# One index column per slot: when GpSimd copies its indices and issues its gathers

## The chip, the cores and the metric

The kernel runs on one core of one Trainium2 chip. The metric is the device time of one execution, in microseconds. Three runs of the kernel before gave a median of 1371.26 us, from 1369.24 to 1378.64. TensorE is called PE below, VectorE DVE, ScalarE ACT, GpSimd POOL and SyncE SP.

## The reference, cut to what matters

The program is one inference step of an encoder layer on 384 tokens (256 of a prompt, 8 streams of 16): a norm, a projection, an mLSTM group beside a sparse attention group, an output projection, and then an expert retrieval, in which the change lies:

```
qp = (x @ w_pq).reshape(T, PEER_HEADS, 2, D_PKEY // 2)
s = jnp.einsum('thcd,hcnd->thcn', qp, subkeys).astype(f32)
s1, i1 = lax.top_k(s[:, :, 0], PEER_TOPK)
s2, i2 = lax.top_k(s[:, :, 1], PEER_TOPK)
...
top_s, sel = lax.top_k(cand, PEER_TOPK)
eidx = jnp.take_along_axis(cidx, sel, axis=-1)
g = jax.nn.softmax(top_s, axis=-1)
u = pu[eidx]
vv = pv[eidx]
a = jax.nn.gelu(jnp.einsum('thkd,td->thk', u, x).astype(f32))
return jnp.einsum('thk,thkd->td', (g * a).astype(vv.dtype), vv)
```

There are 8 heads with 16 experts each, so 128 experts a token, of 16384. A token needs 128 rows of u and 128 rows of v, 1024 floats each.

## The kernel before, in words

The tokens stand in three tiles of 128, one token per partition, taken in the order 2, 0, 1. Everything up to the first routing takes the first 360 us. Then each tile goes through 16 rounds of 8 slots. A slot (`slots[s]`, 128 partitions by 2048 floats) takes, by one indirect DMA, one expert row for each of the 128 tokens, u beside v, 8 KB each, from `peer_uv` in HBM. There are 8 slots, and one gather fills each slot in each round: 3 x 16 x 8 = 384 gathers.

What happens to a slot, by engine:

- POOL copies the indices from `eidx` into a small tile, and issues the gather (`gather`, lines 555 to 577). Its descriptors are made by POOL's software.
- DVE waits for the landing and makes the dot of u with the token, line 1499, `experts`. Between the rounds of the first tile and at the start of the second, DVE also does the routing of later heads and tiles (`routing_steps`: searches on lines 1432 to 1442, pairs, expert indices on lines 1471 to 1492). A step stands behind a round's eight dots, in program order.
- ACT makes the gelu (L731), multiplies by the gate (L733) and writes a diagonal matrix of the weights (L736), and counts `diag_ok`.
- PE waits for the diagonal and multiplies it with the v half, 4 matmuls per slot in float32 as the profile counts them (L1068), accumulating in two banks; it counts `used`. In the first tile's rounds PE also makes the queries of the other two tiles (L1060) and their scores (L1042, L1051).

After a tile's 16 rounds, DVE adds the sum to the residual, norms it (L1505 to L1512), and SP writes it out.

The order of POOL's work is that of its program: `gather` is called for the very first round with `first=True`, unrolled, and then in a loop over rounds. In it stand two groups of four slots (HALF = 4). A group begins with a wait for `diag_ok`, the fourth diagonal of the same group one round ago; by then the issue of the four old gathers, which read the same index tile, is long past. Then one copy of four columns into `isl[g]` follows, and a wait for that copy. Then for each slot come a wait for `used` (the slot's matmuls of the round before), a product of one column by zeros into `pad`, and the issue. In the first round the waits are for the banks' last uses of the memory in which the slots lie (`slot_after`).

Of the kernel before, what the change touches and what calls it, by code (L numbers as in the profile page):

```python
# [12 lines left out]
U32 = mybir.dt.uint32  # L13
ALU = mybir.AluOpType
# [29 lines left out]
SLOTS = 8  # L44
HALF = SLOTS // 2
ROUNDS = HK // SLOTS
# [98 lines left out]
def encoder_kernel(nc, d):  # L145

    plan = psum_plan()
    index = {n: i for i, (n, _) in enumerate(plan)}
    assert len(index) == len(plan)
    CC, NCONST = const_columns()  # L150

    with ExitStack() as ctx:
# [3 lines left out]
        def sem(name):  # L156
            return ctx.enter_context(nc.semaphore(name))

        def at(lo, *shape, parts=P, p0=0):
            n = 1  # L160
            for s in shape:
                n *= s
            assert lo + n <= 52992
            v = arena[p0:p0 + parts, lo:lo + n]
            names = "abcd"[:len(shape)]
            if len(shape) > 1:
                v = v.rearrange(f"p ({' '.join(names)}) -> p {' '.join(names)}",
                                **{c: s for c, s in zip(names[1:], shape[1:])})
            return v

        def over(ap, dim, n):

            v = ap.unsqueeze(dim)
            shape = list(v.shape)
            shape[dim] = n
            return v.broadcast_to(shape)
# [37 lines left out]
        o = CONST + NCONST  # L214
# [81 lines left out]
        o = SM  # L296
# [12 lines left out]
        eidx = at(o + 2176, NT, HK).bitcast(U32)  # L309
        aslot = at(o + 2560, SLOTS)  # L310
        gslot = at(o + 2568, SLOTS)
        wslot_e = at(o + 2576, SLOTS)
        isl = [at(o + 2584 + HALF * g, HALF).bitcast(U32) for g in range(2)]
        pad = at(o + 2592, 1 + SLOTS)
        diag = at(o + 2608, SLOTS, P)
        o += 2608 + SLOTS * P
        assert o <= wslot_at[3]
# [3 lines left out]
        slot_after = ["y11"] * 4 + ["qq3"] * 2 + ["qq7"] * 2  # L321
        slots = [at(a, 2 * DM) for a in slot_at]
# [59 lines left out]
        hn_ok = sem("hn_ready")  # L382
        idx_ok = sem("experts_ready")
        isl_ok = sem("index_slots_ready")
        landed = [sem(f"row_landed_{s}") for s in range(SLOTS)]
        used = sem("rows_used")
        a_ok = sem("dots_ready")
# [2 lines left out]
        diag_ok = sem("diagonals_ready")  # L390
# [4 lines left out]
        def n_read(name, eng):  # L395
            return sum(e == eng for _, e in plan[:index[name] + 1])

        def filled(eng, name):

            eng.wait_ge(filled_s, index[name] + 1)  # L400

        def was_read(eng, name):

            e = plan[index[name]][1]
            eng.wait_ge(read_v if e == "V" else read_a, n_read(name, e))
# [96 lines left out]
        @block.gpsimd  # L502
        def _(pool):
            chain = [0]

            def link(ins):
                chain[0] += 1
                ins.then_inc(p_chain, 1)
                pool.wait_ge(p_chain, chain[0])

            nc.gpsimd.memset(qbd, 0.0)
            nc.gpsimd.memset(qibd, 0.0).then_inc(zeros_p, 1)
            nc.gpsimd.memset(mv1[:, :, :, DH:DX], 1.0).then_inc(mv_ones, 1)
            was_read(pool, "xT21")
            filled(pool, "xT21")
            nc.gpsimd.memset(qdf, 0.0).then_inc(zeros_p, 1)

            pool.wait_ge(mv_ones, 1)
            was_read(pool, "mv2")
            pool.wait_ge(wkm_ok, 1)  # L520
            pool.wait_ge(state_in, 16)
            for h in range(HM):
                if h:
                    filled(pool, f"CN{h - 1}2")
                for t in range(2):
                    nc.gpsimd.tensor_tensor(vw[:, NB + t, :], mv1[:, t, h, :],  # L526
                                            cols[:, 2, t, h:h + 1].broadcast_to([P, DX]), ALU.mult)
                nc.gpsimd.tensor_tensor(vw[:, 0:NB, :], over(mv1[:, 2, h, :], 1, NB),
                                        over(wkm[:, h, :], 2, DX), ALU.mult).then_inc(vw_ok, 1)
                filled(pool, f"NUM{h}")  # L530
                was_read(pool, "decay")
                nc.gpsimd.tensor_tensor(CT[:, h], CT[:, h], over(decb[:, h, :], 2, DX), ALU.mult).then_inc(ct_ok, 1)  # L532

            pool.wait_ge(ml_done, 1)
            nc.gpsimd.memset(kbd, 0.0)
            nc.gpsimd.memset(pnf, 0.0).then_inc(pn0_ok, 1)
            link(nc.gpsimd.memset(ikbd, 0.0))
            was_read(pool, "small")
            was_read(pool, "ak3")

            pool.wait_ge(kidx_in, 16)
            nc.gpsimd.tensor_copy(kiT2[:, :, PAST:LK],
                                  ikT2[:, PROMPT:T].rearrange("p (b t) -> p b t", b=NB)).then_inc(kt_ok, 1)
            pool.wait_ge(cache_in, 16 * JP)
            nc.gpsimd.tensor_copy(KT[:, :, :, PAST:LK],
                                  akT[:, :, PROMPT:T].rearrange("p j (b t) -> p j b t", b=NB)).then_inc(kt_ok, 1)
            pool.wait_ge(kt_ok, 2)

            for e in range(2):
                r = slice(64 * e, 64 * e + 64)  # L550
                link(nc.gpsimd.tensor_copy(ikbd[r, e, :], ikT2[r, 0:PROMPT]))
                nc.gpsimd.tensor_copy(kbd[r, :, e, :], akT[r, :, 0:PROMPT]).then_inc(kbd_ok, 1)
                pool.wait_ge(kbd_ok, e + 1)


            def gather(n, t, i, first):

                done = n * ROUNDS + i
                for g in range(2):
                    if not first:  # L560

                        pool.wait_ge(diag_ok, done * SLOTS - SLOTS + HALF * g + HALF)
                    nc.gpsimd.tensor_copy(isl[g], eidx[:, t, bass.ds(i * SLOTS + HALF * g, HALF)]).then_inc(isl_ok, 1)  # L563
                    pool.wait_ge(isl_ok, done * 2 + g + 1)
                    for s in range(HALF):
                        if first:
                            if slot_after[HALF * g + s]:
                                filled(pool, slot_after[HALF * g + s])
                        else:

                            pool.wait_ge(used, done * SLOTS - SLOTS + HALF * g + s + 1)

                        k = 1 + HALF * g + s
                        nc.gpsimd.tensor_tensor(pad[:, k:k + 1], pad[:, 0:1], pad[:, 0:1], ALU.mult)  # L574
                        nc.gpsimd.indirect_dma_start(  # L575
                            slots[HALF * g + s], None, d["peer_uv"],
                            bass.IndirectOffsetOnAxis(ap=isl[g][:, s:s + 1], axis=0)).then_inc(landed[HALF * g + s], 16)

            for n, t in enumerate(ORDER):
                for part, (u, head, heads) in enumerate(PARTS):  # L580
                    if u != t:
                        continue
                    pool.wait_ge(idx_ok, part + 1)
                    if part == 0:
                        link(nc.gpsimd.memset(pad[:, 0:1], 0.0))  # L585
                        gather(n, t, 0, True)
                    per_head = PK // SLOTS
                    with pool.Fori(max(head * per_head, int(part == 0)), (head + heads) * per_head) as i:
                        gather(n, t, i, False)
# [1074 lines left out]
```

## Time and profile before

| | |
|---|---|
| median of three runs | 1371.26 us (1369.24 to 1378.64) |
| profiled execution | 1376.4 us, of which the span of instructions is 1374.6 us |
| PE busy | 1155.5 us, 84% |
| DVE busy | 799.4 us, 58% |
| ACT busy | 463.8 us, 34% |
| POOL busy | 678.0 us, 49%, 898 instructions |
| gathers (queue of software DMAs) | 402.68 MB of 454.86 MB |

Busy time is time in which an instruction of the engine runs; waits, semaphore and register instructions are not in it. Shares are of the whole span and average over stages that differ. "Idle before" is idle time of the engine just ahead of an instruction, with the one whose end seems to have released it. PEclk is the clock that was granted to PE, 1.00 for its high level of 2.4 GHz, 0.50 for the low one of 1.2 GHz. The DMA share is the mean over the core's 16 DMA engines; it can come out slightly above 1.

### The profile page before, as it was taken

How to read it: one execution, taken by the hardware profiler on the slowest of the kernel's cores; microseconds unless marked ns; L12 is line 12 of the kernel's file. 1: busy time of each engine (PE TensorE's matmuls, PEld its weight loads, DVE VectorE, ACT ScalarE, POOL GpSimd, SP SyncE). 2: the span in 40 equal slices, each digit the busy share in tenths (PEclk: the TensorE clock that was granted, in tenths of full speed). 3: DMA queues.
4: the chain of work that ended last, by engine and by line, in shares of the span. 5: the costliest groups of instructions: out<-in, count | busy, mean ns of one | idle time of the engine just before them, and what ended most of it. 6: DMA issues, size and time to landing. Idle time of an engine off the chain costs nothing.

```text
span 1374.6 us, 12457 instructions
## 1 busy us (share of the span) xinstructions
PE 1155.5 (84%) x3320; PEld 557.0 (41%) x3320; DVE 799.4 (58%) x1837; ACT 463.8 (34%) x1355; POOL 678.0 (49%) x898
## 2 busy tenths in 40 slices
PE   6999899999999997778767778788777877777776
PEld 4546555577855553333323333222222322222222
DVE  4005534866656777878778786455555544455444
ACT  2101200320242433433324343443444444444443
POOL 0002112000255556566655666767776777767772
PEclk9999999989999999798997889999998999999999
DMA  8321528432489999999998999999999999999996
GB/s 316 120 80 62 105 52 295 190 130 116 172 341 384 373 378 422 374 421 386 403 421 338 421 374 407 417 417 422 422 422 422 423 422 422 422 413 422 422 421 268
DMA packets 68825, 454.86 MB, mean 331 GB/s; under 512 B 7241, under 2 KB 14765, under 8 KB 17329
## 3 DMA queue, kind: packets, MB, share of 16 engines
q0 software_dynamic: 55296, 402.68, 71.2%
q1 hardware_dynamic: 12656, 48.60, 10.3%
q10 hardware_dynamic: 832, 3.08, 0.7%
q8 instruction: 20, 0.33, 0.1%
q14 instruction: 21, 0.16, 0.0%
HBM read 446.62 MB, written 7.71 MB: 331 GB/s over the span
## 4 chain that ended last, share of the span: by engine, by line
PE 36%; DMA 30%; POOL 12%; issue 9%; DVE 8%; ACT 4%; POOLq 1%; DVEq 0%; ACTq 0%; SPq 0%
DMA arena<-in_peer_uv,arena 29%; PE ps L1068 10%; PE ps L802 7%; POOL arena L575 7%; PE ps L808 4%; PE ps L1060 4%; POOL arena L574 3%; PE ps L922 3%; POOL arena L563 2%; PE ps L1042 2%; DVE arena L1499 2%; ACT arena L736 1%; ACT arena L733 1%; PE ps L1015 1%; DVE arena L1261 1%
## 5 line engine op out<-in xcount | busy, mean ns | idle before, releaser
L1068 PE MATMUL ps<-arena 128*128 128x512 f32 x1536 | 755.9, 633 | 190.6 <-ACT arena L736 190.4
L1499 DVE CUSTOM_DVE_ANT_0 arena<-arena 128x1024 f32<-128x1024 f32 x384 | 468.1, 1231 | 374.3 <-DMA arena<-in_peer_uv,arena 373.4
L1068 PEld LDWEIGHTS ps<-arena 128*128 128x128 f32 x1536 | 285.7, 198 | 655.6 <-ACT arena L736 369.0
L575 POOL DMA_INDIRECT arena<-in_peer_uv,arena x384 | 445.5, 1160 | 85.9 <-issue 76.9
L731 ACT ACTIVATE arena<-arena 128x1 f32<-128x1 f32 x384 | 77.3, 201 | 469.4 <-DVE arena L1499 466.1
L563 POOL COPY arena<-arena 128x4 uint32 (+1 forms) x96 | 71.9, 749 | 223.6 <-ACT arena L736 223.2
L736 ACT ACTIVATE arena<-arena 128x128 f32<-128x128 f32 x384 | 154.2, 402 | 12.5
L574 POOL TENSOR_TENSOR arena<-arena 128x1 f32<-128x1 f32 x384 | 132.3, 344 | 34.2 <-POOL arena L563 14.5
L733 ACT ACTIVATE arena<-arena 128x1 f32 (+1 forms) x384 | 113.0, 294 | 32.5
L802 PE MATMUL ps<-arena 128*128 128x384 f32 (+1 forms) x336 | 112.2, 492 | 0.0
L616 ACT ACTIVATE arena<-ps 128x512 f32<-128x512 f32 (+2 forms) x63 | 30.6, 511 | 239.5 <-PE ps L1060 70.7
L802 PEld LDWEIGHTS ps<-arena 128*128 128x128 f32 (+1 forms) x336 | 63.5, 192 | 44.0 <-issue 2.2
L585 POOL MEMSET arena<- 128x1 f32 x1 | 0.1, 98 | 140.9 <-DVE arena L1488 140.9
L808 PE MATMUL ps<-arena 128*128 128x512 f32 x144 | 62.5, 592 | 0.0
L1060 PE MATMUL ps<-arena 128*128 128x256 f32 x256 | 56.2, 379 | 0.9 <-ACT arena L616 0.9
L526 POOL TENSOR_TENSOR arena<-arena 128x129 f32<-128x129 f32 x8 | 3.0, 401 | 106.8 <-DVE arena L1189 88.7
L1060 PEld LDWEIGHTS ps<-arena 128*128 128x128 f32 x256 | 48.6, 190 | 9.4 <-issue 1.9
L922 PE MATMUL ps<-arena 128*128 128x512 f32 x96 | 43.3, 603 | 1.6 <-ACT arena L616 1.6
L731 ACT ACT_TABLE_LOAD x33 | 42.3, 1283 | 0.6
L808 PEld LDWEIGHTS ps<-arena 128*128 128x128 f32 x144 | 27.1, 190 | 32.8 <-issue 32.5
L532 POOL TENSOR_TENSOR arena<-arena 128x1032 f32<-128x1032 f32 x4 | 7.6, 1909 | 62.9 <-PE ps L886 62.9
L1499 DVE DVE_READ_ACCUMULATOR2_ANT arena<- 128x1 f32 x384 | 30.5, 80 | 0.0
(230 smaller groups left out, 710.1 us busy)
## 6 DMA issues: line engine op xcount, KB each, us to landing
arena<-in_w_in SPq DMA_DIRECT2D x8, 2048.0 KB, 7.6
arena<-in_w_pq SPq DMA_DIRECT2D x4, 2048.0 KB, 9.9
arena<-in_peer_uv,arena POOLq DMA_INDIRECT x384, 9.6
arena<-in_w_out SPq DMA_DIRECT2D x3, 1024.0 KB, 7.0
arena<-in_state_C ACTq DMA_DIRECT2D x1, 2064.0 KB, 10.3
out_new_C_s<-arena SPq DMA_DIRECT2D x1, 2064.0 KB, 6.6
arena<-in_cache_k SPq DMA_DIRECT2D x4, 512.0 KB, 7.0
arena<-in_cache_v SPq DMA_DIRECT2D x1, 2048.0 KB, 16.5
```

What stands on the lines that cost most here:

```text
L563: nc.gpsimd.tensor_copy(isl[g], eidx[:, t, bass.ds(i * SLOTS + HALF * g, HALF)]).then_inc(isl_ok, 1)
L574: nc.gpsimd.tensor_tensor(pad[:, k:k + 1], pad[:, 0:1], pad[:, 0:1], ALU.mult)
L575: nc.gpsimd.indirect_dma_start(slots[HALF * g + s], None, d["peer_uv"], bass.IndirectOffsetOnAxis(ap=isl[g][:, s:s + 1], axis=0)).then_inc ...
L731: act.activation(gslot[:, s:s + 1], aslot[:, s:s + 1], ACT.Gelu_apprx_tanh).then_inc(ge_ok, 1)
L733: act.activation(wslot_e[:, s:s + 1], gflat[:, t, bass.ds(i * SLOTS + s, 1)], ACT.Copy, scale=gslot[:, s:s + 1]).then_inc(w_ok, 1)
L736: act.activation(diag[:, s, :], ident, ACT.Copy, scale=wslot_e[:, s:s + 1]).then_inc(diag_ok, 1)
L802: last = mm(b[0:m, 0:T], w[:, k, lo:lo + m], xnT[:, k, :], start=k == 0, stop=k == KC - 1)
L808: last = mm(b, xnT[:, k, P * t:P * t + P], w[:, k, :], start=k == 0, stop=k == KC - 1)
L922: last = mm(b, mixT[:, k, P * t:P * t + P], wout[i][k], start=k == ks[0], stop=k == ks[-1])
L1060: last = mm(b[:, 0:PROMPT], w[:, k, P * g:P * g + P], xnT[:, k, 0:PROMPT], start=k == 0, stop=k == KC - 1)
L1068: last = mm(ps[:, BANKS + half, :], diag[:, s, :], slots[s][:, DM + 512 * half:DM + 512 * half + 512], start=first and s == 0, stop=final ...
L1499: v.tensor_tensor_reduce(slots[s][:, 0:DM], slots[s][:, 0:DM], hn[:, t, :], 1.0, 0.0, ALU.mult, ALU.add, aslot[:, s:s + 1]).then_inc(a_ok, 1)
```

## The change

The two index tiles of four columns become eight of one column, one for each slot. The zero column `pad` and its products are gone, with the memset that fills it. In `gather` the group level disappears: each slot waits for its own `used` count, then copies its one column, waits for that copy, increments a new semaphore that nobody waits for, and issues its gather. The wait for `diag_ok` is gone from POOL. In the first round the order is the same, behind `slot_after`.

```diff
-        isl = [at(o + 2584 + HALF * g, HALF).bitcast(U32) for g in range(2)]
-        pad = at(o + 2592, 1 + SLOTS)
+        isl = [at(o + 2584 + s, 1).bitcast(U32) for s in range(SLOTS)]
...
+        issued = sem("gathers_begun")
...
-                done = n * ROUNDS + i
-                for g in range(2):
-                    if not first:
-
-                        pool.wait_ge(diag_ok, done * SLOTS - SLOTS + HALF * g + HALF)
-                    nc.gpsimd.tensor_copy(isl[g], eidx[:, t, bass.ds(i * SLOTS + HALF * g, HALF)]).then_inc(isl_ok, 1)
-                    pool.wait_ge(isl_ok, done * 2 + g + 1)
-                    for s in range(HALF):
-                        if first:
-                            if slot_after[HALF * g + s]:
-                                filled(pool, slot_after[HALF * g + s])
-                        else:
-
-                            pool.wait_ge(used, done * SLOTS - SLOTS + HALF * g + s + 1)
-
-                        k = 1 + HALF * g + s
-                        nc.gpsimd.tensor_tensor(pad[:, k:k + 1], pad[:, 0:1], pad[:, 0:1], ALU.mult)
-                        nc.gpsimd.indirect_dma_start(
-                            slots[HALF * g + s], None, d["peer_uv"],
-                            bass.IndirectOffsetOnAxis(ap=isl[g][:, s:s + 1], axis=0)).then_inc(landed[HALF * g + s], 16)
+
+                done = (n * ROUNDS + i) * SLOTS
+                for s in range(SLOTS):
+                    if first:
+                        filled(pool, slot_after[s])
+                    else:
+                        pool.wait_ge(used, done - SLOTS + s + 1)
+                    nc.gpsimd.tensor_copy(isl[s], eidx[:, t, bass.ds(i * SLOTS + s, 1)]).then_inc(isl_ok, 1)
+                    pool.wait_ge(isl_ok, done + s + 1)
+                    pool.sem_inc(issued, 1)
+                    nc.gpsimd.indirect_dma_start(
+                        slots[s], None, d["peer_uv"],
+                        bass.IndirectOffsetOnAxis(ap=isl[s], axis=0)).then_inc(landed[s], 16)
...
-                        link(nc.gpsimd.memset(pad[:, 0:1], 0.0))
```

## Rows read from the trace of the kernel before

**Rows 1.** Stretches: bounds, length, busy us per engine, PEclk, DMA share, GB/s.

```profile
500.00:860.00 360.00, 281.12 (x600) 118.98 (x598) 279.46 (x769) 136.58 (x421) 220.97 (x308) 0.88 0.97 397
860.00:1340.00 480.00, 381.22 (x769) 132.12 (x770) 242.58 (x392) 204.94 (x603) 345.19 (x434) 0.99 1.01 421
```

**Rows 2.** Timeline around 1200 us, DVE and PE: start, duration, what, idle before.

```profile
1200.21 1.23 DVE L1499 CUSTOM_DVE_ANT_0 arena<-arena 128x1024 f32<-128x1024 f32 x1 [1.24 <-DMA arena<-in_peer_uv,arena]
...
1202.59 1.98 PE L1068 MATMUL ps<-arena 128*128 128x512 f32 x4 [0.50 <-ACT arena L736]
...
1205.17 1.23 DVE L1499 CUSTOM_DVE_ANT_0 arena<-arena 128x1024 f32<-128x1024 f32 x1 [1.24 <-DMA arena<-in_peer_uv,arena]
```

**Rows 3.** Chain of waits in order of time, 448 to 485 us: start, us, what.

```profile
448.48 14.00 PE ps L1068 x32
462.48 6.92 PE ps L1060 x32
470.72 14.00 PE ps L1068 x32
```

**Rows 4.** Stretches of 10 us with low DMA share, columns as in rows 1.

```profile
490.00:500.00 10.00, 8.14 (x29) 4.72 (x28) 7.75 (x13) 7.30 (x23) 2.30 (x4) 1.00 0.77 321
560.00:570.00 10.00, 10.00 (x23) 4.46 (x22) 8.60 (x19) 5.60 (x13) 8.53 (x12) 0.94 0.73 269
730.00:740.00 10.00, 10.00 (x23) 4.38 (x22) 9.82 (x21) 6.81 (x16) 8.59 (x10) 0.91 0.44 164
```

**Rows 5.** Timeline at 366 us and around 1200 us, POOL.

```profile
366.13 0.19 POOL L563 COPY arena<-arena 128x4 uint32<-128x4 uint32 x1
...
1200.51 1.78 POOL L575 DMA_INDIRECT arena<-in_peer_uv,arena  x1 [0.15 <-issue]
...
1205.19 1.25 POOL L563 COPY arena<-arena 128x4 uint32 x1 [1.55 <-ACT arena L736]
1206.61 0.20 POOL L574 TENSOR_TENSOR arena<-arena 128x1 f32<-128x1 f32 x1 [0.16 <-POOL arena L563]
1207.27 0.98 POOL L575 DMA_INDIRECT arena<-in_peer_uv,arena  x1 [0.47 <-issue]
```

**Rows 6.** Page, costliest groups, POOL's: count, busy us, mean ns, idle before.

```profile
L575 POOL DMA_INDIRECT arena<-in_peer_uv,arena x384 | 445.5, 1160 | 85.9 <-issue 76.9
...
L563 POOL COPY arena<-arena 128x4 uint32 (+1 forms) x96 | 71.9, 749 | 223.6 <-ACT arena L736 223.2
...
L574 POOL TENSOR_TENSOR arena<-arena 128x1 f32<-128x1 f32 x384 | 132.3, 344 | 34.2 <-POOL arena L563 14.5
```

**Rows 7.** One tile's instructions: the gathers from 900 to 1300 us.

```profile
DMA to landing us min/median/max: 7.1/8.5/11.9
```

**Rows 8.** Stretch of 1 us at 558 us, columns as in rows 1.

```profile
558.00:559.00 1.00, 1.00 (x2) 0.34 (x1) 1.00 (x1) 0.87 (x3) 0.00 (x0) 0.50 1.04 434
```

**Rows 9.** Timeline around the low slice at 560 us.

```profile
555.56 16.80 PE L1068 MATMUL ps<-arena 128*128 128x512 f32 x32 [8.50 <-ACT arena L736]
559.13 13.22 PE L1068 MATMUL ps<-arena 128*128 128x512 f32 x28
...
559.11 1.16 POOL L563 COPY arena<-arena 128x4 uint32 x1 [7.85 <-ACT arena L736]
560.17 1.23 DVE L1499 CUSTOM_DVE_ANT_0 arena<-arena 128x1024 f32<-128x1024 f32 x1
560.43 1.02 POOL L574 TENSOR_TENSOR arena<-arena 128x1 f32<-128x1 f32 x1 [0.16 <-POOL arena L563]
561.60 0.98 POOL L575 DMA_INDIRECT arena<-in_peer_uv,arena  x1
```

**Rows 10.** Timeline around 732 us, POOL.

```profile
733.03 1.80 POOL L575 DMA_INDIRECT arena<-in_peer_uv,arena  x1
```

**Rows 11.** Timeline around 667 us, POOL.

```profile
667.05 1.49 POOL L575 DMA_INDIRECT arena<-in_peer_uv,arena  x1 [1.79 <-issue]
```

**Rows 12.** Stretch of 10 us at 660 us, columns as in rows 1.

```profile
660.00:670.00 10.00, 10.00 (x21) 4.24 (x20) 6.39 (x11) 4.90 (x16) 4.51 (x8) 0.83 0.96 388
```

## The prediction

> **What bounds the kernel now.** I read the time by stretches first. From 860 to 1340 us the DMA engines are busy at 1.01 and move 421 GB/s, while PE, DVE and POOL have idle time; from 500 to 860 us it is 0.97 and 397 GB/s [rows 1]. A gather moves 128 rows of 8 KB, 1.049 MB; at 421 GB/s that is 2.49 us. The starts of DVE's dots confirm it: two dots later is 4.96 us, 2.48 us each [rows 2]. So the last third is bound by the transfers. In the chain of waits the rounds from about 380 to 492 us are PE's instead: 14.0 us of expert matmuls, 6.92 us of prompt queries, and round again after 22.2 us, where eight gathers need 19.9 us [rows 3]. Between 490 and 860 us both are interrupted by routing work on DVE: there the reader should see five slices of 10 us in which the DMA share is only 0.44 to 0.79 (three of them are shown) [rows 4]. The missing rate is (421 - 397) / 421 x 360 us = 20.5 us from 500 to 860 us, and (421 - 321) / 421 x 10 = 2.4 us in the slice from 490: 23 us is all that better feeding of the transfers can give.
>
> **What POOL does.** In the bound stage a gather takes 1.79 us of POOL's 2.49 (345.19 us of 480 [rows 1], over 193 gathers). The group's copy starts when ACT's fourth diagonal is there; the product and the issue follow [rows 5]. The issue takes 0.97 us, or 1.78 us when it begins inside a DVE dot: the issue that began at 1200.51 ended 0.85 us after the dot that ended at 1201.44. The copy that began at 1205.19 ended at 1206.44, with the dot of 1205.17 to 1206.40 [rows 2, 5]. So each POOL instruction that meets a dot waits for its end. The Trainium skill (SBUF — State Buffer, two separate sides) says the same more strongly: VectorE with two SBUF inputs and a GpSimd operation that reads SBUF take one port pair as an exclusive lock. By that rule alone all products, copies and issues would wait whenever DVE is busy; here issues beside DVE's searches still take 0.97 us, so the dots are what counts.
>
> **The change, part by part.** The sum is against the profiled execution (1376.4 us, span 1374.6), which lies 5 us above the median of the runs, 1371.3; I take the difference from the median.
>
> (1) Removed: 384 products, mean 344 ns, 132 us of POOL [rows 6]. Added: 288 more copies (384 instead of 96). No copy of one column is in the trace. The nearest row is the product of one column, 0.20 us free of a dot [rows 5]; the copy of four columns takes 0.19 us free and 1.25 us in a dot [rows 5], mean 749 ns [rows 6]. I take 0.20 free and the rest of the dot where it meets one, since it has the same shape as the product. One copy then replaces one product and the old copies drop out: POOL's work falls slightly. In the bound stage this is worth nothing, POOL not being the limit; the transfers cover it. Bounds: 0 to the price of rival A.
>
> (2) Each copy is now awaited before its issue: 0.17 us from copy to product and 0.46 us from product to issue at the group's head [rows 5]. I put both on every gather: 0.20 + 0.63 + 0.98 = 1.81 us of POOL, plus at most the rest of one dot. The increment of the new semaphore has no row; between 0 and the 0.46 us gap, taken inside that gap. Does POOL keep up? A dot takes 1.23 us of the 2.48; the freed slot comes 4.36 us after its dot's start (dot from 1200.21, matmuls from 1202.59 to 1204.57 [rows 2]), which is 1.88 us into the next dots' period. The copy ends at 2.2, the issue begins at 2.5 to 2.9, waits for the dot to 3.7 (1.23 of the next period), and ends at 4.6, 0.85 later. That is 2.1 into the next period: the next slot's copy starts there, and the same repeats. POOL locks to the period and does not stretch it. The slot is out of the queue for 4.4 + 2.7 = 7.1 us of 19.9, so about five gathers stay queued. Time from issue to landing, 8.5 us now [rows 7], should rise to about 12. The stage gains and loses 0 us.
>
> (3) The new copy waits for its own slot's matmuls instead of the fourth diagonal. Queued behind that wait are only the later slots' copies and gathers, which become free in the same order. Nobody but the gathers waits for POOL here. In the PE stage the transfers have slack already: 0, unless PE's cover goes, and it is 2.3 us a round (22.2 - 19.9). The part that can pay is the holes. A hole begins when all eight slots have landed and DVE is still in a routing step; no slot is free, so earlier issuing can't move its start. Its end can move. In the hole at 560 us the PE clock is granted at 0.50 [rows 8], its low level of 1.2 GHz, after PE had been idle for 8.5 us, so slot 0's four matmuls, begun at 555.56, end only about when the fifth begins, at 559.13. The old copy, released by the fourth diagonal, starts at 559.11 [rows 9]. The old wait thus costs nothing; what goes is the product of 1.02 us. New: copy until 560.25, issue begun at 560.45 to 560.75 inside the dot of 560.17 to 561.40, ended 0.85 later at 562.25, against 561.60 + 0.98 = 562.58 [rows 9]: 0.35 us. The holes of 644 and 816 us have the same pattern, that of 498 (PE warm) gives about 0.5. In the long one at 730 us copy and product each met a dot, and the issue of 733.03 met a third and took 1.80, to 734.83 [rows 10]; without the product the issue meets the dot before and ends at about 733.7: 1.1 us. Slots 1 to 7 follow at PE's 1.7 us, faster than 2.48, so they change nothing. Sum 3 x 0.35 + 0.5 + 1.1 = 2.7 us. Bounds for these: 0, and all 23 us.
>
> (4) At 667 us a thin stretch: slot 1's issue begins 1.79 us late by the row, share 0.96 in that slice [rows 11, 12]. With that row's gap gone, 1.3 us (388 of 421 GB/s for two such slices gives 1.6 at most). First gather of all: product and memset gone, 0.3 us earlier at 360 us, under PE's rounds, 0.
>
> Sum: -2.7 - 1.3 = **-4.0 us**, so 1367 us (profiled execution 1372). What a measurement can tell from no change is about 1%, 13.7 us; this is below it.
>
> **The rivals.** A: **POOL becomes the limit**, slower. Place: every gather after 500 us. With the means of today, copy 0.749, waits 0.17 + 0.46, issue 1.160 [rows 5, 6], a gather takes 2.54 us of POOL, 0.055 above the transfers' 2.48; over about 330 gathers +18 us, 1390 us. If copy and issue each met a whole dot it would be 1.25 + 0.63 + 1.78 = 3.66 us, but a longer period has more free time, so that can't hold. The point from which it decides is 2.48 us of POOL per gather. Against it: the phases of part 2, where only one of the two meets a dot. For it: an unseen cost of waits on the sequencer. The Trainium skill (GPSIMD Engine Reference, Performance pitfalls for Q7 kernels) speaks against the change: many small reads, one per gather index, should be batched, since each pays about 102 cycles; its estimate is 288 x 85 ns = 24 us of POOL. The trace agrees in kind: a product of one column takes as long as a copy of four, 0.20 and 0.19 us [rows 5]; but POOL has the time. Chance of A 0.12.
>
> B: **the deeper queue fills the holes**, faster. If the holes came from slots that sat free behind the group's fourth diagonal (up to 3 x 2.48 = 7.4 us), most of the 23 us would return: 1348 with all, 1356 with two thirds. For it: POOL's idle time before the copies is charged to ACT's diagonals, 223 us [rows 6]. Against: in the holes all eight slots are landed, and the low clock delays the first free one. Chance 0.13.
>
> C: **nothing changes**, 1371, the wait for the slot having always been the later one where it counts; it lies in the forecast's band. Forecast with C: 0.75.
>
> **How the numbers follow.** Forecast and C spread over 1362 to 1376, with the runs' own spread (1369 to 1379) to 1380. The range reaches to B's 1356 and to part of A: 1356 to 1384. Faster by over 1% (below 1357.5) 0.12, slower by over 1% (above 1385) 0.11, within 1% 0.77.
>
> **What would show it.** 384 copies of about 0.2 or up to 1.2 us and no product; POOL waiting for PE's matmuls, not for diagonals; issue to landing near 12 us; DMA share still 1.01 from 900 us on, dots 2.48 us apart; the five holes at their old places and hardly shorter. I am wrong if dots in the last stage are further apart than 2.5 us (A), if POOL has no idle time there, or if the slices of 0.44 and 0.73 fill up (B).

## The result, and the profile after

The changed kernel is slightly slower. 17 runs of it have a median of 1384.06 us (1376.51 to 1391.11); 17 of the kernel before, in the same jobs, 1375.59 us (1369.24 to 1379.74). The ratio is 1.0065, 95% interval [1.0043, 1.0087]: +0.65%, about 9 us. The forecast was -4 us, within 1% of no change. It was right that the change is small; the sign was wrong, and the median lies just above the upper end of the range, 1384. Part of the distance to the forecast of 1367 us is the starting point: it was taken from three runs with a median of 1371.3, and the 17 runs lie in two clusters, eight from 1369.2 to 1371.7 and eight from 1377.6 to 1379.7, with one between them that happens to be the median.

The profiled execution of the changed kernel took 1378.85 us, span 1377.0, close to the one of before. The two spans compare badly, because the work ahead of the gathers, which nobody changed, was faster in it. The reader should measure from the first gather's issue to DVE's addition at the end of each tile. In the changed kernel (start, duration, what):

```profile
353.61 1.14 POOL L568 DMA_INDIRECT arena<-in_peer_uv,arena  x1 [0.96 <-POOL arena L565]
...
717.95 0.69 DVE L1497 TENSOR_TENSOR arena<-arena,ps 128x512 f32<-128x512 f32 x1
...
1044.69 0.69 DVE L1497 TENSOR_TENSOR arena<-arena,ps 128x512 f32<-128x512 f32 x1 [3.16 <-PE ps L1060]
...
1369.50 0.69 DVE L1497 TENSOR_TENSOR arena<-arena,ps 128x512 f32<-128x512 f32 x1 [3.16 <-PE ps L1060]
```

And in the kernel before:

```profile
360.89 1.16 POOL L575 DMA_INDIRECT arena<-in_peer_uv,arena  x1 [0.43 <-issue]
...
720.32 0.69 DVE L1505 TENSOR_TENSOR arena<-arena,ps 128x512 f32<-128x512 f32 x1
...
1046.83 0.69 DVE L1505 TENSOR_TENSOR arena<-arena,ps 128x512 f32<-128x512 f32 x1 [3.16 <-PE ps L1068]
...
1367.00 0.69 DVE L1505 TENSOR_TENSOR arena<-arena,ps 128x512 f32<-128x512 f32 x1 [3.16 <-PE ps L1068]
```

Before, the three tiles take 359.4, 326.5 and 320.2 us, 1006.1 in all. After, they take 364.3, 326.7 and 324.8 us, 1015.9 in all. The gather phase is 9.8 us longer, the size of the difference of the medians; it is lost in the first and the last tile.

The stretches that answer to [rows 1] show less moved in both:

```profile
500.00:860.00 360.00, 274.23 (x590) 115.09 (x588) 275.13 (x738) 136.52 (x421) 210.24 (x270) 0.90 0.97 393
860.00:1340.00 480.00, 378.30 (x763) 131.03 (x764) 239.21 (x388) 203.18 (x597) 317.76 (x381) 0.99 1.01 417
```

393 in place of 397 GB/s, and 417 in place of 421 in a stage that the transfers should bound. The page's groups of POOL answer to [rows 6]:

```profile
L568 POOL DMA_INDIRECT arena<-in_peer_uv,arena x384 | 432.6, 1127 | 318.6 <-POOL arena L565 162.8
...
L565 POOL COPY arena<-arena 128x1 uint32 (+1 forms) x384 | 186.0, 484 | 203.1 <-DVE arena L1480 135.7
```

POOL is less busy than before (646.9 us for 678.0), yet idle time of 318.6 us has appeared in front of the issues, where it was 85.9. It is 0.83 us a gather. It is time between the end of the copy and the start of the issue, and it is no spare time: POOL cannot use it. The steady state around 1201 us, which answers to [rows 2] and [rows 5]:

```profile
1201.08 0.96 POOL L568 DMA_INDIRECT arena<-in_peer_uv,arena  x1 [0.81 <-PE ps L1060]
1201.38 1.98 PE L1060 MATMUL ps<-arena 128*128 128x512 f32 x4 [0.49 <-ACT arena L728]
1201.50 1.23 DVE L1491 CUSTOM_DVE_ANT_0 arena<-arena 128x1024 f32<-128x1024 f32 x1 [1.26 <-DMA arena<-in_peer_uv,arena]
1202.04 0.72 POOL L565 COPY arena<-arena 128x1 uint32 x1
...
1203.57 0.95 POOL L568 DMA_INDIRECT arena<-in_peer_uv,arena  x1 [0.81 <-PE ps L1060]
```

The copy starts the moment the last issue ends (1201.08 + 0.96 = 1202.04), so its slot had been free already. The copy meets the dot and ends with it (1202.76 against 1202.73). Then 0.81 us pass, then the issue. 0.72 + 0.81 + 0.96 = 2.49 us: POOL has no slack at all, though its least time is 0.19 + 0.81 + 0.96 = 1.96 us. As forecast it has locked to the dots' period. What the forecast missed is what this means: a POOL that makes exactly one issue per dot never makes up for a delay by itself.

The delays can be seen in the time from issue to landing, which the text takes as the depth of the queue (min, median, max of the gathers between 900 and 1300 us, then between 900 and 920, 940 and 960, 1210 and 1230):

```profile
DMA to landing us min/median/max: 5.5/7.8/9.9
...
DMA to landing us min/median/max: 9.3/9.3/9.4
...
DMA to landing us min/median/max: 6.8/6.8/6.8
...
DMA to landing us min/median/max: 5.5/5.8/5.9
```

It was forecast to rise from 8.5 to 12 us; it fell to 7.8. It mostly stays at one level for tens of us and drops at single places, from 9.3 to 6.8 us at 943 and from 7.8 to 5.8 at 1211. Between them it came back to 7.8: by 980 us, behind a slice of 10 us at 388 GB/s, and again by 1260, behind the slices at 393 and 380 shown below. So the depth does come back, but while it does the transfers lose time. The two drops come from a pause in front of an issue:

```profile
1207.02 0.71 POOL L565 COPY arena<-arena 128x1 uint32 x1
1211.12 0.96 POOL L568 DMA_INDIRECT arena<-in_peer_uv,arena  x1 [3.39 <-PE ps L1060]
1212.08 0.68 POOL L565 COPY arena<-arena 128x1 uint32 x1
1213.59 0.96 POOL L568 DMA_INDIRECT arena<-in_peer_uv,arena  x1 [0.82 <-PE ps L1060]
```

3.39 us in place of 0.81. It stands before gathers number 114, 220 and 326 of 384. The kernel before has a shorter pause before numbers 114 and 326 too ([rows 11] is the first; the second is 1.48 us). There POOL had slack: the slice from 1210 us fell to 388 GB/s, and the next four are at 421 to 426. Here the queue is down to 5.8 us afterwards, and the transfers run thin:

```profile
1230.00:1240.00 10.00, 7.54 (x16) 2.41 (x14) 4.78 (x8) 3.57 (x12) 6.74 (x9) 1.00 1.01 408
1240.00:1250.00 10.00, 7.93 (x16) 2.71 (x16) 4.97 (x8) 4.04 (x12) 6.74 (x9) 1.00 1.00 393
1250.00:1260.00 10.00, 6.57 (x14) 2.41 (x15) 4.27 (x7) 3.55 (x12) 6.74 (x9) 1.00 1.00 380
```

With the two slices before them (370 and 402 GB/s) that is (52 + 20 + 14 + 29 + 42) / 422 x 10 = 3.7 us. The kernel before loses 0.7 us in the same five slices, so this stretch explains about 3 us of the last tile's 4.6. The share of each tile differs from one execution to the next: in the trace of e6 below, the changed kernel with its loop written out, the three tiles take 363.4, 327.9 and 322.1 us.

In the first tile the refill after a hole is a part of it. The one that answers to [rows 9]:

```profile
550.00 16.92 PE L1060 MATMUL ps<-arena 128*128 128x512 f32 x32 [8.50 <-ACT arena L728]
...
553.95 0.76 POOL L565 COPY arena<-arena 128x1 uint32 x1 [6.79 <-PE ps L1060]
...
555.52 1.15 POOL L568 DMA_INDIRECT arena<-in_peer_uv,arena  x1 [0.81 <-POOL arena L565]
...
557.78 1.35 POOL L568 DMA_INDIRECT arena<-in_peer_uv,arena  x1 [0.81 <-POOL arena L565]
...
570.31 1.13 POOL L568 DMA_INDIRECT arena<-in_peer_uv,arena  x1 [0.81 <-POOL arena L565]
```

The first issue stands 5.52 us after PE's start, where it was 6.04 (555.56 to 561.60): 0.5 us gained, as forecast (0.35). But the seventh issue is at 570.31, six spacings of 2.47 us; before, all eight were out from 561.60 to 574.09, seven spacings of 1.78. The queue is refilled no faster than the transfers drain it. The slices from 550 to 590 us are at 298, 382, 398 and 380 GB/s, 5.5 us short of 422; before, the two slices at 269 and 409 from 560 us were 3.9 us short.

### The profile page after: what moved, and what is told of

Same layout as the page of the kernel before. It is cut to its first block, busy times and chain, and to the rows that moved or that the text cites. A ratio compares the mean times of both kernels' runs of the same rounds, so it can differ in the third digit from the quotient of the medians.

```text
span 1377.0 us, 13306 instructions
## 1 busy us (share of the span) xinstructions
PE 1147.1 (83%) x3320; PEld 549.6 (40%) x3320; DVE 796.3 (58%) x1837; ACT 463.7 (34%) x1355; POOL 646.9 (47%) x801
## 4 chain that ended last, share of the span: by engine, by line
PE 37%; DMA 20%; POOL 16%; DVE 11%; issue 11%; ACT 4%; POOLq 2%; SPq 0%; ACTq 0%; DVEq 0%
DMA arena<-in_peer_uv,arena 18%; PE ps L1060 12%; POOL arena L568 12%; PE ps L794 7%; PE ps L800 4%; POOL arena L565 4%; PE ps L1052 4%; DVE arena L1491 4%; PE ps L914 3%; PE ps L1034 2%; ACT arena L728 1%; DMA arena<-in_w_out 1%; ACT arena L725 1%; DVE arena L1253 1%; DVE arena L1475 1%
## 5 line engine op out<-in xcount | busy, mean ns | idle before, releaser
L568 POOL DMA_INDIRECT arena<-in_peer_uv,arena x384 | 432.6, 1127 | 318.6 <-POOL arena L565 162.8
L565 POOL COPY arena<-arena 128x1 uint32 (+1 forms) x384 | 186.0, 484 | 203.1 <-DVE arena L1480 135.7
L1034 PE MATMUL ps<-arena 128*128 128x128 f32 x256 | 29.3, 275 | 0.7 <-ACT arena L608 0.7
```

The costliest lines, as they stand in the source:

```text
L565: nc.gpsimd.tensor_copy(isl[s], eidx[:, t, bass.ds(i * SLOTS + s, 1)]).then_inc(isl_ok, 1)
L568: nc.gpsimd.indirect_dma_start(slots[s], None, d["peer_uv"], bass.IndirectOffsetOnAxis(ap=isl[s], axis=0)).then_inc(landed[s], 16)
L1034: last = mm(b[:, P * g:P * g + P], w[:, k, P * g:P * g + P], xnT[:, k, PROMPT:T], start=k == 0, stop=k == KC - 1)
```

## Experiments

Theory 1: an awaited small instruction directly ahead of each issue costs 0.81 us, so POOL needs 1.97 us a gather where it needed 1.35, and locked to DVE's dots it cannot refill the queue. Theory 2: the slot by slot order is what hurts. Theory 3: only the stages ahead differ. Each kernel was timed beside the kernel before, and ratios are to it.

The 1.35 us of theory 1 can be read in the kernel before, from one issue to the next inside a group (1199.16 to the issue of [rows 5] at 1200.51):

```profile
1199.16 0.97 POOL L575 DMA_INDIRECT arena<-in_peer_uv,arena  x1 [0.15 <-issue]
1200.15 0.21 POOL L574 TENSOR_TENSOR arena<-arena 128x1 f32<-128x1 f32 x1
```

**e2: the kernel before, with each product awaited.**

```diff
-                        nc.gpsimd.tensor_tensor(pad[:, k:k + 1], pad[:, 0:1], pad[:, 0:1], ALU.mult)
+                        nc.gpsimd.tensor_tensor(pad[:, k:k + 1], pad[:, 0:1], pad[:, 0:1], ALU.mult).then_inc(pad_ok, 1)
+                        pool.wait_ge(pad_ok, done * SLOTS + k)
+                        pool.sem_inc(issued, 1)
```

> The kernel before, with each product awaited (its own semaphore) before the issue behind it; the grouped wait for the diagonals and the grouped copies stay. Theory 1 (each gather's awaited small instruction puts 0.81 us between itself and the issue, so POOL needs at least 0.20 + 0.81 + 0.96 = 1.97 us a gather where it needed 1.35, and cannot catch up after a disturbance): slower than before by 5 to 12 us, about as the changed kernel or a little more, since the issues also begin late. Theory 2 (what costs is the earlier, slot by slot issue, through another phase against DVE's dots or a shallower queue): within 3 us of before. Theory 3 (the runs differ by the stages ahead of the gathers only): within 3 us.

1400.93 us, ratio 1.0184 [1.0131, 1.0237], +25 us. Nothing of the order was changed, and it is slower than the changed kernel. The sign is theory 1's, the size two to five times the 5 to 12 us that I wrote. A likely reason, not tested by itself: the copies of four stand beside the 384 awaited products here, and the issues of a group still begin late. POOL's rows show the same 0.81 us:

```profile
1101.38 0.97 POOL L579 DMA_INDIRECT arena<-in_peer_uv,arena  x1 [0.81 <-POOL arena L576]
1102.35 0.80 POOL L576 TENSOR_TENSOR arena<-arena 128x1 f32<-128x1 f32 x1
1103.96 0.97 POOL L579 DMA_INDIRECT arena<-in_peer_uv,arena  x1 [0.81 <-POOL arena L576]
```

**e3: the changed kernel, with the grouped wait put back.**

```diff
+                        if s % HALF == 0:
+                            pool.wait_ge(diag_ok, done - SLOTS + s + HALF)
                         pool.wait_ge(used, done - SLOTS + s + 1)
```

> The changed kernel, with the wait for the group's fourth diagonal put back ahead of the first and fifth slot of each round; one awaited copy per slot stays. Theory 1: as slow as the changed kernel or slower, +8 to +20 us over before, since late bursts are then issued at 1.97 us or more each. Theory 2: the grouping is what kept before fast, so this comes back to before, within 3 us. Theory 3: within 3 us.

1382.39 us, ratio 1.0062 [1.0029, 1.0095]: equal to the changed kernel. Theory 2 is out: the late order does not bring the time back. Theory 3 is out by this run, by e2 and by the length of the gather phase above. Nor does the early order give anything here that can be measured.

**e4: the kernel before without its product.**

```diff
-                        k = 1 + HALF * g + s
-                        nc.gpsimd.tensor_tensor(pad[:, k:k + 1], pad[:, 0:1], pad[:, 0:1], ALU.mult)
+                        pool.sem_inc(issued, 1)
```

> The kernel before without its 384 products and the zero column; a semaphore increment stands in their place, grouped copies and grouped waits stay. The issue has about 0.15 to 0.2 us less or one dot less before it. Theory 1: POOL needs about 1.1 us a gather, so equal to before or faster by up to 5 us. Theory 2: equal to before within 3 us. If the product itself were of use (it spaces the issues), slower by 5 us or more.

1372.59 us, ratio 0.9988 [0.9962, 1.0015]: no change. Taking the product out and putting the increment in comes to nothing that can be measured.

**e1: no copy at all.** POOL's loop is written out, and the gather reads its indices from the table.

```diff
-                    nc.gpsimd.tensor_copy(isl[s], eidx[:, t, bass.ds(i * SLOTS + s, 1)]).then_inc(isl_ok, 1)
-                    pool.wait_ge(isl_ok, done + s + 1)
                     pool.sem_inc(issued, 1)
...
-                        bass.IndirectOffsetOnAxis(ap=isl[s], axis=0)).then_inc(landed[s], 16)
+                        bass.IndirectOffsetOnAxis(ap=eidx[:, t, i * SLOTS + s:i * SLOTS + s + 1], axis=0)).then_inc(landed[s], 16)
...
-                    with pool.Fori(max(head * per_head, int(part == 0)), (head + heads) * per_head) as i:
+                    for i in range(max(head * per_head, int(part == 0)), (head + heads) * per_head):
```

> The changed kernel with POOL's loops over rounds written out, so that each gather reads its indices straight from the table of all indices: no copy, no wait for it; the issue waits only for its slot's matmuls. Theory 1: POOL needs about 1.0 to 1.2 us a gather, five gathers are queued, time from issue to landing rises to about 12 us, and the time falls below the kernel before by 3 to 8 us (about 1366). Theory 2 (early issue costs): +5 to +12 us over before, as the changed kernel. Theory 3: equal to before within 3 us.

1373.86 us, ratio 0.9994 [0.9966, 1.0022]. The awaited copy's cost is gone, with the slot by slot order kept, as theory 1 says. The further gain of 3 to 8 us did not come, although the queue filled up:

```profile
DMA to landing us min/median/max: 7.8/14.7/15.9
```

14.7 us of queue in place of 8.5 is worth nothing where 8.5 was already enough. This trace shows one thing more: its issues wait for PE, and they too start 0.8 us after what they wait for. PE's matmuls from 1142.25 end at 1144.23, the issue begins at 1145.05. So the 0.81 us is not special to a copy; but in the changed kernel it comes behind POOL's own work, on every gather.

**e5: each copy made one round ahead.** As many small copies as in the changed kernel (57 a half tile for 64), but the one an issue needs was made a round earlier.

```diff
-                    nc.gpsimd.tensor_copy(isl[s], eidx[:, t, bass.ds(i * SLOTS + s, 1)]).then_inc(isl_ok, 1)
-                    pool.wait_ge(isl_ok, done + s + 1)
+                    if (i + 1) % (4 * PK // SLOTS):
+                        copy_ahead(n, t, i + 1, s, 1)
+                    pool.wait_ge(isl_ok, ready[r, s])
                     pool.sem_inc(issued, 1)
```

> The changed kernel with POOL's rounds written out, two sets of eight index columns, and each copy made one round ahead of its gather (one copy of eight columns at the head of each half tile). As many small copies as in the changed kernel, each slot still issued as soon as it is free, but no issue stands behind a copy that has just been made. Theory 1 (the 0.81 us between an awaited small instruction and the issue): POOL needs about 0.20 + 0.15 + 0.96 = 1.3 us, issue to landing at 10 us or more, time equal to the kernel before within 3 us. Theory 2b (it is the number of small copies and their meetings with DVE's dots, not the awaiting): +5 to +10 us over before.

1373.67 us, ratio 1.0005 [0.9984, 1.0026], issue to landing 14.7 us. So it is the awaiting directly ahead of the issue, not the number of copies. Its timeline shows the same pause as above, and then what the changed kernel lacks:

```profile
1194.04 0.19 POOL L561 COPY arena<-arena 128x1 uint32<-128x1 uint32 x1
1197.25 1.76 POOL L580 DMA_INDIRECT arena<-in_peer_uv,arena  x1 [3.02 <-issue]
1199.02 0.19 POOL L561 COPY arena<-arena 128x1 uint32<-128x1 uint32 x1
1199.37 0.96 POOL L580 DMA_INDIRECT arena<-in_peer_uv,arena  x1 [0.15 <-issue]
1200.33 0.38 POOL L561 COPY arena<-arena 128x1 uint32<-128x1 uint32 x1
1200.87 0.96 POOL L580 DMA_INDIRECT arena<-in_peer_uv,arena  x1 [0.16 <-issue]
...
1202.18 1.80 POOL L580 DMA_INDIRECT arena<-in_peer_uv,arena  x1 [0.15 <-issue]
```

After the pause the next issues follow 2.12, 1.50 and 1.31 us apart, 0.15 us behind their neighbours' copies, and the delay is made up: issue to landing falls to 12.1 us and is back at 14.7 by 1210.

**e6: the changed kernel with POOL's loops written out**, the control for e1 and e5.

```diff
-                    nc.gpsimd.tensor_copy(isl[s], eidx[:, t, bass.ds(i * SLOTS + s, 1)]).then_inc(isl_ok, 1)
+                    nc.gpsimd.tensor_copy(isl[s], eidx[:, t, i * SLOTS + s:i * SLOTS + s + 1]).then_inc(isl_ok, 1)
...
-                    with pool.Fori(max(head * per_head, int(part == 0)), (head + heads) * per_head) as i:
+                    for i in range(max(head * per_head, int(part == 0)), (head + heads) * per_head):
```

> The changed kernel with POOL's loops written out and nothing else: the copies stay, each awaited before its issue. It is the control for the two kernels without loops. Theory 1: as the changed kernel, +6 to +11 us over before, issue to landing near 7.8 us, 0.8 us between copy and issue. If the loop (its branches and register waits) were what costs: equal to before within 3 us.

1383.11 us, ratio 1.0069 [1.0037, 1.0101]: the changed kernel's time. The loop is not the cause.

**e7: a second awaited instruction** between copy and issue.

```diff
                     pool.wait_ge(isl_ok, done + s + 1)
+                    nc.gpsimd.tensor_tensor(pad[:, 1 + s:2 + s], pad[:, 0:1], pad[:, 0:1], ALU.mult).then_inc(pad_ok, 1)
+                    pool.wait_ge(pad_ok, done + s + 1)
                     pool.sem_inc(issued, 1)
```

> The changed kernel with a second awaited small instruction (a product of one column) between copy and issue. POOL's least time a gather goes from 1.97 us to 0.20 + 0.16 + 0.20 + 0.81 + 0.96 = 2.33 us, or 2.98 us if the second wait costs 0.81 us as well. Theory 1: slower again, +20 to +40 us over before in the first case, and about 300 x (2.98 - 2.48) = +150 us in the second, since POOL then is the limit. Theory 2 (early issue or its phase is what costs): as the changed kernel, +6 to +11 us.

1434.27 us by the median, ratio 1.0486 [1.0423, 1.0549]: 60 us slower by medians, 67 by the ratio. The four runs spread widely, from 1410.39 to 1448.30 us, and the trace is that of the fastest. The rows show the first case (issue to issue 2.26 to 2.28 us at the least), since the first wait's successor is a product and starts after 0.08 us; only the issue stands 0.81 us behind:

```profile
1103.26 0.20 POOL L567 COPY arena<-arena 128x1 uint32 x1
1103.54 0.19 POOL L569 TENSOR_TENSOR arena<-arena 128x1 f32<-128x1 f32 x1
1104.55 1.19 POOL L572 DMA_INDIRECT arena<-in_peer_uv,arena  x1 [0.81 <-POOL arena L569]
```

The traced run is 37 us above the median of the kernel before, inside the expected 20 to 40; the three others are 60 to 74 us above, so the size was underestimated. POOL's least time of 2.28 us is still below the transfers' 2.48. The loss grows steeply as the distance between the two shrinks, as far as two points can say it: about 9 us at a least time of 1.97, 37 to 74 at 2.28. The least time alone does not set the loss, though: e2, whose issues inside a group stand 1.99 us apart at the least, lost 25 us. In its first stretch the rate is down to 368 GB/s:

```profile
500.00:860.00 360.00, 258.27 (x548) 107.37 (x547) 267.18 (x728) 127.78 (x395) 236.16 (x379) 0.87 0.96 368
```

**e8, e9 and their repeats: short dots.** In both kernels DVE's dot is cut to 256 columns (a part of the result is left out).

```diff
-                    v.tensor_tensor_reduce(slots[s][:, 0:DM], slots[s][:, 0:DM], hn[:, t, :], 1.0, 0.0,
+                    v.tensor_tensor_reduce(slots[s][:, 0:256], slots[s][:, 0:256], hn[:, t, 0:256], 1.0, 0.0,
```

> The changed kernel with DVE's dots cut to 256 of 1024 columns (the rest of each dot is left out), so a dot takes about 0.4 us in place of 1.23 and seldom holds POOL up. To be compared with the next run, the kernel before cut in the same way. Theory 1, with the dots holding POOL: POOL needs 1.97 us and has 0.5 us a gather to catch up, issue to landing rises to 12 us or more, and the difference between the two cut kernels shrinks from about 9 us to 0 to 4 us. If the awaited copy costs in some other way that has nothing to do with the dots: the difference stays at 7 us or more.

> The kernel before with DVE's dots cut to 256 of 1024 columns in the same way. All theories: a few us faster than the whole kernel before (the holes under DVE's routing are shorter by 0.8 us a slot), 1350 to 1368 us; the transfers bound both. Theory 1: the changed kernel cut in the same way lies 0 to 4 us above this one; otherwise 7 us or more.

> The changed kernel with dots cut to 256 of 1024 columns once more, on the same chip as the kernel before cut in the same way, so that the two are compared directly. Theory 1: 0 to 4 us above it. Otherwise 7 us or more above it.

The changed kernel cut: 1367.22 us, ratio 0.9954 [0.9927, 0.9980] (e8), and 1367.47, 0.9945 [0.9922, 0.9968] (e8b). The kernel before cut (e9): 1361.94, 0.9888 [0.9836, 0.9940], of four runs only. The medians of e8b and e9 are 5.5 us apart: between the two expectations. The traces say where. From 860 to 1340 us both move 422 GB/s, and both take 320.5 to 320.7 us for the last tile, where the whole kernels differ by 4.6. The changed kernel's queue, cut, is 15.1 us deep, that of the kernel before 10.8. In e8b:

```profile
1195.80 0.18 POOL L565 COPY arena<-arena 128x1 uint32 x1 [0.53 <-PE ps L1060]
...
1199.37 0.96 POOL L568 DMA_INDIRECT arena<-in_peer_uv,arena  x1 [3.39 <-issue]
...
1201.35 0.95 POOL L568 DMA_INDIRECT arena<-in_peer_uv,arena  x1 [0.82 <-PE ps L1060]
...
1203.31 0.96 POOL L568 DMA_INDIRECT arena<-in_peer_uv,arena  x1 [0.81 <-POOL arena L565]
```

With a dot of 0.43 us, the issues follow the pause 1.98 and 1.96 us apart: POOL's least time, below 2.48, so the delay is made up (issue to landing falls to 12.6 us and is back at 15.1 by 1210). The pair with more rounds:

> The kernel before with dots cut to 256 of 1024 columns, once more with more rounds, beside the changed kernel cut alike. So far the two lay 5.5 us apart by medians, of 4 and 10 runs; in their last tile both take 320.5 us, and both move 422 GB/s from 860 us on. Theory 1 as it stands (the dots' hold on POOL is what keeps the queue low in the last stage; the slow refill of 1.97 us a gather after each hole costs without them too): a difference of 2 to 6 us remains, all of it before the last tile. If all of the cost hung on the dots: 0 to 2 us.

> The changed kernel with dots cut to 256 of 1024 columns, in the same job. Theory 1 as it stands: 2 to 6 us above the run before this one, issue to landing near 15 us, last tile as long as there. If all of the cost hung on the dots: 0 to 2 us above.

1360.77 us, 0.9893 [0.9861, 0.9924] (e9b, before), and 1363.14 us, 0.9917 [0.9893, 0.9942] (e8c, changed): 2.4 us apart by medians, in the expected 2 to 6. So about 2 to 6 us are left with short dots, against about 9 with whole ones. How the 9 us divide is not settled, since the intervals of the two cut kernels overlap in both jobs. From the first gather's issue to the last addition, which leaves out the work ahead, the two traces of the kernel before, cut, have 997 us and the three of the changed kernel 998 to 1000: 1 to 3 us apart, against 9.8 for the whole kernels. Shown is that the last tile's part goes. That it goes because the dots no longer hold POOL is argued from the spacing of the issues: a short dot also frees its slot 0.8 us earlier, and no run separates the two.

No kernel here that computes the whole result beats the kernel before by more than the measurement can tell. e1, e4 and e5 are level with it.

## Why the prediction was wrong

**Step (1), right.** POOL is less busy with 384 copies than with products and old copies together: 646.9 for 678.0 us. e4 shows that taking the product out is worth nothing.

**Step (2) is the step that failed.** Its arithmetic was that POOL locks to the period, does not stretch it, and that therefore "about five gathers stay queued". The lock came, the queue did not, and the term "the stage gains and loses 0 us" measured +4.6 us in the last tile. I had computed one steady cycle as if each copy found its slot just freed. The real cycle has POOL behind: from 860 to 1340 us 188 of 190 copies start as soon as the issue before them ends, and the depth of the queue is what the last disturbance left, 9.3, 6.8 or 5.8 us, or the 7.8 to which it came back while the transfers lost time. A second fault made it worse: I took the gap to the issue as 0.17 + 0.46 = 0.63 us and left out the 0.20 of the product that ran inside it in [rows 5]. From the copy's end to the issue's start that row reads 0.83, and 0.81 is what every gather now pays. More important, [rows 5] and the rows of the kernel before under the experiments show that the gap is paid at the head of a group alone (0.47 us ahead of that issue, 0.15 ahead of one inside a group), so that the kernel before could issue every 1.35 us. This spare speed, 1.35 against 2.48, is what the change spent. e2 shows the loss with the awaiting alone, e1 and e5 show it gone without.

**Step (3), half right.** PE's idle time in the hole did not change (8.50 us in both), the first issue came 0.5 us earlier where 0.35 was forecast, and the first slot did come late with PE's clock granted at 0.50. "Slots 1 to 7 follow at PE's 1.7 us" was wrong: they follow at POOL's 2.47 us. This hole and its refill cost about 1.5 us more than before, and the first tile, where a gain of 2.7 us was forecast for the holes, took 4.9 us more.

**Step (4), wrong.** The 1.79 us pause of [rows 11] belongs to gather number 114, not to the grouping. It stayed, at 3.40 us, so the 1.3 us did not come.

**What holds POOL.** The prediction took the rule of the Trainium skill (SBUF — State Buffer, two separate sides) to mean that POOL waits whenever DVE is busy, and concluded that only the dots count. The rule names DVE instructions with two SBUF inputs (or in a two-port mode), and the trace of the changed kernel agrees with it: a copy that meets a routing instruction with two inputs ends with it (1.07 us), one that meets a reduction with one input takes 0.19 us. In the same trace all six copies that began in such an instruction of two inputs and 1024 columns ended with it, and the five issues 0.82 to 0.83 us behind it; the five copies that began in the reductions, and those beside the searches, took 0.19 us:

```profile
563.17 1.23 DVE L1472 TENSOR_TENSOR arena<-arena 128x1024 f32<-128x1024 f32 x1
563.36 1.07 POOL L565 COPY arena<-arena 128x1 uint32 x1
...
565.89 1.22 DVE L1477 TENSOR_REDUCE arena<-arena 128x64 f32<-128x1024 f32 x1
566.36 0.19 POOL L565 COPY arena<-arena 128x1 uint32 x1
```

So the routing's instructions of two inputs hold POOL as well, and they stand in the stretch behind the hole at 550 us.

**The rivals.** A, POOL as the limit, had the right sign and the right engine. Its price (+18 us) came from means of blocked instructions, and its point of decision, a mean of 2.48 us, was wrong: the changed kernel loses at a least time of 1.97 us, e7 loses 37 to 74 us at 2.28. By these runs what counts most is how far POOL's unhindered time lies below the transfers', since catching up is done with the difference. B, a deeper queue, is refuted by e1 and e5: 14.7 us deep and no gain; a hole opens when all slots are full. The batching rule of the Trainium skill (GPSIMD Engine Reference, Performance pitfalls for Q7 kernels) pointed the right way but not to the cause: it is stated for read commands of code on GpSimd's own cores, and e5 has nearly as many small copies as the changed kernel and no loss.

## What to carry to other kernels

An engine that issues transfers needs spare speed, not only a mean below the transfers' rate: compare its unhindered time per issue with the transfers' time, and ask what refills the queue after a stall. Do not put a just made, awaited result directly ahead of an issue; make it a round, or some slots, earlier. When an engine locks to another's period in a computed steady state, take it as a warning: it has nothing with which to make up for a delay, and here the depth came back only while the bound stage lost time.

## What the runs showed of the hardware

- An indirect DMA's issue on POOL starts 0.81 us after the end of an awaited instruction on POOL (0.80 to 0.83 in 380 of 384), and about as long after PE's awaited matmuls (e1). A product starts 0.08 us (e7) or 0.16 us (before) after an awaited copy. An issue behind a product that nobody awaits starts after 0.15 us (0.47 us at the head of a group).
- Ahead of gathers 114 and 326 of 384 POOL pauses in every trace, and ahead of 220, 106 after the first and before the last of them, in all but the kernels that issue by groups and await no product (before, e4, e9). Where the copy or product is awaited, the issue comes 3.39 us after it in place of 0.81, 2.6 us more; in the kernel before it comes after 1.79 and 1.48 us in place of 0.15. The traces do not show its cause, and no run tested it.
- A DVE instruction with two inputs holds a copy on POOL until its own end (six of six copies, 1.07 us the one shown), one with one input does not (0.19 us).
- The first gather's issue falls at 353.6 us in one trace and at 360.9 in another, with the same work ahead. Whether this is what makes the two clusters of the kernel before, around 1370 and 1379 us, was not tested.
